# Further rounds of an expert with 32 slots instead of 64, in four column groups and four row groups of TensorE's array

## The chip, the cores and the metric

The kernel runs on one core of one Trainium2 chip. The metric is device time in microseconds (us) of one execution. Three runs of the kernel before gave 1126.19 (the median), 1116.86 and 1128.22 us.

## The reference

The program is one inference step of a two-layer decoder trunk on 320 tokens: 256 of a prompt and 64 of a sample group, with the same weights. Layer 0 has a Conformer convolution module and layer 1 multi-head latent attention. Each layer ends in a mixture of 16 experts, and each token goes to two of them:

```python
def moe(x, r_w, r_b, w1, w3, w2):
    t = x.reshape(-1, D_MODEL)                       # D_MODEL = 1024
    aff = jax.nn.sigmoid((t @ r_w).astype(jnp.float32))
    ...                                              # best group of 4, then the top 2 experts in it
    gates = ...                                      # 0 but for the two chosen experts of a token
    out = jnp.zeros(t.shape, jnp.float32)
    for e in range(N_EXPERTS):                       # 16
        h = jax.nn.silu(t @ w1[e]) * (t @ w3[e])     # 1024 -> 512, twice
        out = out + gates[:, e:e + 1] * (h @ w2[e]).astype(jnp.float32)
    return out.astype(x.dtype).reshape(x.shape)
```

All of it is in float32. The routing of these inputs, counted with the reference's own functions for prompt and sample together, gives the experts of layer 0 28, 43, 43, 52, 49, **65**, 53, 41, 52, 33, 15, 42, 34, 30, 40, 20 tokens, and those of layer 1 53, **68**, 35, 50, 55, 57, 36, 22, 49, 30, 19, 48, 35, 23, 40, 20.

## The kernel before

The kernel computes an expert on gathered tokens, `C = 64` slots at a time, with one instruction stream per engine written by hand and semaphores between them. **The first round** of an expert takes its first 64 tokens: POOL gathers the rows of x from HBM by an indirect DMA, PE turns them (`turn_rows`, L931, into the bank `TURN`), ACT copies them to SBUF (L692), PE makes the up products with w1 and w3 (`up`, L944: the product with w1 lies in partitions 0 to 63 of the bank `UP`, that with w3 in 64 to 127), ACT takes silu of the one half (L697), DVE multiplies by the other (L1353), PE turns the hidden rows (L931), DVE copies them (L1357), PE makes the down product (`down`, L952, into the bank `DOWN`: the columns 0 to 511 of the result in partitions 0 to 63, the others in 64 to 127), and DVE copies the result (L1362). Two experts share one put product (`put`, L987): a one-hot matrix with the gates in it, turned by PE, times the results, added onto the residual that stays in five PSUM banks (`TOTAL`) through all 16 experts.

**A further round** takes the next 64 tokens of an expert that has more. The routing on DVE counts the rounds of every expert (L1310 to L1326, the table `rounds`), and each engine's stream has after each expert a branch on that number and a loop (`further`, L999 on PE). The rounds use TensorE's matmuls of the first round on buffers of their own, with the same weights, and end with their own put product (L1022 and L1023) whose left side is one expert's one-hot rows in partitions 64 to 127. In the round everything is one chain: turn (L931), ACT copy (L710), up (L944), silu (L713), product (L1372), turn of the hidden rows (L931) and of the one-hot matrix (L1013), copy (L1374), down (L952), two copies (L1378), put (L987). Its gather (L556) is issued long before.

**What sets the order around it.** The weights of an expert are 6.3 MB: w1 and w3 (two DMAs, L416), w2 (one DMA, L419). They have two buffers, and a third one for expert 2 alone. SP's stream issues the DMAs of expert e+2 when the buffer of expert e is free, further rounds included: `load_over` (L436 to L442) waits for the last up product of e before it issues w1 and w3, and for the last down product before w2. All go into one queue in order. PE waits at L955 (`w13_ready`) for w1 and w3.

## Time and profile before

| | |
|---|---|
| runs | 1116.86, 1126.19, 1128.22 us |
| span of the profiled execution | 1117.9 us (the page gives no other time of its own) |
| PE busy | 980.2 us, 88% of the span |
| DVE, ACT, POOL busy | 336.2, 167.1, 104.3 us |
| chain that ended last | PE 71%, DMA 12%, DVE 8%, ACT 3% |
| read from HBM | 260.04 MB, of them about 200 MB expert weights |

A row of a group of instructions has the line in the kernel, engine, operation, what it writes and reads, the shape and the count, then the summed busy time and the mean duration of one.
### The profile page before, as it was taken

The numbers are of one execution on the slowest core, as the hardware profiler recorded it, in microseconds if no ns is written. First come the engines' busy times: TensorE is split into PE (matmuls) and PEld (weight loads), VectorE is DVE, ScalarE is ACT, GpSimd is POOL, SyncE is SP. The second block draws the span as 40 slices with busy tenths as digits, with TensorE's granted clock in tenths as the row PEclk, the third lists the DMA queues.
The fourth block names the chain that finished last, engine by engine and source line by source line (L and its number), as shares of the span: only waits on it lengthen the run. The fifth ranks groups of instructions, "written<-read, shape, count | busy, mean of one in ns | idle before, by whom it ended". The sixth has DMA issues, their size and how long they took to land.

```text
span 1117.9 us, 14216 instructions
## 1 busy us (share of the span) xinstructions
PE 980.2 (88%) x4754; PEld 485.2 (43%) x4755; DVE 336.2 (30%) x792; ACT 167.1 (15%) x327; POOL 104.3 (9%) x196
## 2 busy tenths in 40 slices
PE   3989979799989998968998888889798999989993
PEld 2756534543323343325655555444543334323331
DVE  1554445421121221142224433213521121211215
ACT  1000031211011110012122322220111011111001
POOL 2051000101000000014100023000010000000000
PEclk9989989699999999998898989989698999999997
DMA  8485261999969999978203110557385399999991
GB/s 215 121 291 155 59 258 58 341 364 367 367 233 319 377 376 378 392 252 279 73 6 96 53 55 24 190 203 285 131 278 197 146 324 376 382 379 373 385 353 48
DMA packets 131621, 267.18 MB, mean 239 GB/s; under 512 B 7386, under 2 KB 39158, under 8 KB 131555
## 3 DMA queue, kind: packets, MB, share of 16 engines
q1 hardware_dynamic: 121200, 237.75, 60.2%
q0 software_dynamic: 5392, 12.60, 4.3%
q10 hardware_dynamic: 4979, 16.15, 4.0%
q8 instruction: 33, 0.54, 0.2%
q14 instruction: 17, 0.14, 0.0%
HBM read 260.04 MB, written 7.15 MB: 239 GB/s over the span
## 4 chain that ended last, share of the span: by engine, by line
PE 71%; DMA 12%; DVE 8%; ACT 3%; SPq 2%; issue 2%; ACTq 0%; DVEq 0%
PE bank L944 19%; DMA w<-in_e_w 9%; PE bank L952 9%; PE wide L987 4%; PE bank L877 4%; PE bank L770 3%; PE bank L931 3%; PE wide L877 2%; PE wide L770 2%; PE wide L1708 2%; PE bank L786 2%; DMA w<-in_state_conv 2%; PE bank L1585 2%; DMA dbuf<-in_a_w_pw 2%; PE bank L1686 2%
## 5 line engine op out<-in xcount | busy, mean ns | idle before, releaser
L944 PE MATMUL bank<-w,dbuf 128*64 128x512 f32 x1024 | 234.0, 610 | 14.4 <-DMA w<-in_e_w 11.5
L944 PEld LDWEIGHTS bank<-w,dbuf 128*64 128x64 f32 x1024 | 78.9, 141 | 163.0 <-issue 160.8
L952 PE MATMUL bank<-w,dbuf 128*64 128x512 f32 x512 | 129.9, 653 | 11.0 <-DVE dbuf L1357 10.4
L1362 DVE COPY dbuf<-bank 64x512 f32<-64x512 f32 x64 | 44.1, 689 | 164.6 <-PE bank L952 164.2
L1353 DVE TENSOR_TENSOR dbuf<-dbuf,bank 64x512 f32<-64x512 f32 x32 | 22.1, 690 | 204.4 <-ACT dbuf L697 204.4
L697 ACT ACTIVATE dbuf<-bank 64x512 f32<-64x512 f32 x32 | 18.9, 591 | 418.2 <-PE bank L944 418.2
L952 PEld LDWEIGHTS bank<-w,dbuf 128*64 128x64 f32 x512 | 42.5, 148 | 81.4 <-issue 81.1
L987 PE MATMUL wide<-dbuf,ukT 128*128 128x512 f32 (+1 forms) x144 | 70.3, 615 | 6.0 <-DVE dbuf L1378 3.0
L931 PEld LDWEIGHTS bank<-ident,dbuf 64*128 64x128 f32 x476 | 41.3, 160 | 50.9 <-issue 41.7
L931 PE MATMUL bank<-ident,dbuf 64*128 64x64 f32 x476 | 50.6, 244 | 9.9 <-DVE dbuf L1362 3.4
L540 POOL COPY idx_col<-idx 64x1 int32 (+1 forms) x32 | 5.7, 179 | 572.5 <-PE bank L931 389.5
L527 POOL DMA_DIRECT2D w<-in_cache_kpe x64 | 34.3, 536 | 224.0 <-PE bank L1686 123.3
L770 PE MATMUL bank<-xT,dbuf 128*128 128x320 f32 x128 | 39.5, 471 | 3.8 <-DMA dbuf<-in_a_w_pw 3.8
L987 PEld LDWEIGHTS wide<-dbuf,ukT 128*128 128x128 f32 (+1 forms) x144 | 24.7, 189 | 30.5 <-issue 19.2
L770 PE MATMUL wide<-xT,dbuf 128*128 128x320 f32 x128 | 35.4, 435 | 0.0
L770 PEld LDWEIGHTS bank<-xT,dbuf 128*128 128x128 f32 x128 | 26.7, 210 | 16.0 <-DMA dbuf<-in_a_w_pw 4.3
L543 POOL DMA_INDIRECT dbuf<-x_rows,idx_col x32 | 29.9, 936 | 11.3 <-issue 11.3
L786 PE MATMUL bank<-w,ukT 128*32 128x256 f32 x512 | 29.3, 380 | 0.0
L770 PEld LDWEIGHTS wide<-xT,dbuf 128*128 128x128 f32 x128 | 24.1, 190 | 10.9 <-issue 1.2
L877 PE MATMUL bank<-dbuf,w 128*128 128x512 f32 (+1 forms) x64 | 23.4, 635 | 6.0 <-ACT w L620 6.0
L1357 DVE COPY dbuf<-bank 128x256 f32<-128x256 f32 x32 | 13.6, 425 | 40.2 <-PE bank L931 39.5
L692 ACT ACTIVATE dbuf<-bank 128x512 f32<-128x512 f32 x32 | 19.1, 597 | 42.3 <-PE bank L931 42.3
(352 smaller groups left out, 1115.1 us busy)
## 6 DMA issues: line engine op xcount, KB each, us to landing
w<-in_e_w SPq DMA_DIRECT2D x90, 2048.0 KB, 20.2
dbuf<-in_a_w_pw SPq DMA_DIRECT2D x16, 512.0 KB, 5.8
w<-u_rows SPq DMA_DIRECT2D x32, 142.0 KB, 3.0
dbuf<-in_a_w_pw ACTq DMA_DIRECT2D x1, 4096.0 KB, 17.8
dbuf<-in_e_w SPq DMA_DIRECT2D x2, 2048.0 KB, 14.9
w<-in_cache_ckv SPq DMA_DIRECT2D x32, 128.0 KB, 2.7
dbuf<-in_cache_ckv SPq DMA_DIRECT2D x32, 128.0 KB, 2.1
dbuf<-in_b_w_o SPq DMA_DIRECT2D x2, 2048.0 KB, 7.8
```

The source lines that it names most:

```text
L527: pool.dma_start(cpe[p % 2][:, bass.ds(it * 4 + n, 1)].rearrange("p o r -> p (o r)"), src)\
L543: nc.gpsimd.indirect_dma_start(xg[s], None, x_rows[l], bass.IndirectOffsetOnAxis(ap=idx_col[s][:], axis=0))\
L770: last = nc.tensor.matmul(B[2 * s + h][:, 0:T], pw1[s][:, k, h], xT[:, k], start=(k == 0), stop=(k == KD - 1))
L786: last = nc.tensor.matmul(B[6 + j % 2][32 * g:32 * g + 32, 0:SEQ], tap_w[j % 2][:, g, q], copies[j % 2][:, g, 4 * q:4 * q + SEQ], start=(q ...
L877: last = nc.tensor.matmul(dst, left[:, k, t0:t0 + m], w_out[:, k, h * 512:(h + 1) * 512], start=(k == 0), stop=(k == KD - 1))
L931: last = nc.tensor.matmul(bank[:, k * C:(k + 1) * C], src[:, k * P:(k + 1) * P], ident[r0:r0 + C, r0:r0 + C], start=True, stop=True, is_tr ...
L944: last = nc.tensor.matmul(bank[n * C:(n + 1) * C], x[:, k], w[n][k], start=(k == 0), stop=(k == KD - 1))
L952: last = nc.tensor.matmul(bank[n * C:(n + 1) * C], h[:, k], w[k][:, n * 512:(n + 1) * 512], start=(k == 0), stop=(k == 3))
L987: last = nc.tensor.matmul(TOTAL[i][h], left[:, t0:t0 + m], rows[:, h * 512:(h + 1) * 512], start=False, stop=stop)
L1362: last = V.tensor_copy(y_pair[s * C:(s + 1) * C, h * 512:(h + 1) * 512], DOWN[h * C:(h + 1) * C, :])
L1585: last = nc.tensor.matmul(B[h % 2][:, 0:T], wuq[:, k, h * 192:h * 192 + NOPE], cqT[:, k], start=(k == 0), stop=(k == 3))
L1686: last = nc.tensor.transpose(key_bank(n)[0:(P if n < 8 else ROPE), j * P:(j + 1) * P], src, ident[:])
```

## The change

A further round holds `H = 32` slots; the first round keeps 64. An expert with 65 to 96 tokens has one further round as before, one with 97 to 128 has two where it had one.

- **Up** (`up_more`): the 512 columns of w1 and of w3 are cut in halves, and each of the four quarters goes into a column group of its own, 32 of the array's columns wide: 32 matmuls of 256 moving columns instead of 16 of 512. w1's product lies in partitions 0 to 63 (half a in 0 to 31, half b in 32 to 63), w3's in 64 to 127.
- **Silu and product** are then on 64 x 256 instead of 64 x 512, the copy before the up product on 128 x 256 instead of 128 x 512.
- **Turn of the hidden rows** takes 2 matmuls instead of 4. DVE writes each turned block twice, side by side, so that the down product has 64 columns on its left side as before and gives each of its 32 rows twice.
- **Copy of the result**: the result's 512-column halves lie in partitions 0 to 63 and 64 to 127, each row twice, and are copied by one 128 x 512 instruction instead of two of 64 x 512.
- **Put** (`put_rows_more`): the one-hot matrix is built four times side by side (128 x 128 instead of 128 x 64, three instructions), turned into 128 partitions and copied, and each matmul of the put product takes 32 rows of it in a row group of its own; token tiles 0 and 1 and the two halves of the result have four different ones.
- **Routing** on DVE: up to 8 further rounds instead of 4 are counted, which is 4 more small instructions in each of two loops, and the matrices of slots are 6 x 8 x 16 instead of 6 x 4 x 16 (and 6 x 32 instead of 6 x 64).
- **The gather** of a further round has 32 rows.

```diff
+            def turn_more():
+                for k in range(KD):
+                    last = nc.tensor.matmul(TURN[:, k * H:(k + 1) * H], xg_more[:, k * P:(k + 1) * P], ident[0:H, 0:H],
+                                            start=True, stop=True, is_transpose=k > 0)
+                return last
+            def up_more(w):
+                for k in range(KD):
+                    for q in range(4):
+                        n, lo = q // 2, q % 2 * (FE // 2)
+                        last = nc.tensor.matmul(UP[q * H:(q + 1) * H, 0:FE // 2], xe_more[:, k],
+                                                w[n][k][:, lo:lo + FE // 2], start=(k == 0), stop=(k == KD - 1))
+                return last
+            def turn_hidden_more():
+                for c in range(2):
+                    last = nc.tensor.matmul(UP[:, c * C:(c + 1) * C], hid_more[:, c * P:(c + 1) * P],
+                                            ident[C:2 * C, C:2 * C], start=True, stop=True, is_transpose=c > 0)
+                return last
+            def down_more(w):
+                for k in range(4):
+                    for n in range(2):
+                        last = nc.tensor.matmul(DOWN[n * C:(n + 1) * C],
+                                                hT_more[:, k % 2 * 2 + k // 2].rearrange("p r t -> p (r t)"),
+                                                w[k][:, n * 512:(n + 1) * 512], start=(k == 0), stop=(k == 3))
+                return last
+            def put_rows_more():
+                for i, (t0, m) in enumerate(TILES):
+                    for h in range(2):
+                        r0 = (2 * h + i % 2) * H
+                        nc.tensor.matmul(TOTAL[i][h], put_more[r0:r0 + H, t0:t0 + m], y_more[r0:r0 + H],
+                                         start=False, stop=False)
...
-                        turn_rows(TURN, xg_more, KD).then_inc(m_turned, 1)
+                        turn_more().then_inc(m_turned, 1)
                         pe.wait_ge(m_copied, first + c)
-                        up(xe_more, UP, W13[w]).then_inc(m_up, 1)
+                        up_more(W13[w]).then_inc(m_up, 1)
                         pe.wait_ge(m_hid, first + c)
-                        turn_rows(UP, hid_more, 4, C).then_inc(m_ht, 1)
+                        turn_hidden_more().then_inc(m_ht, 1)
...
                         pe.wait_ge(m_htc, first + c)
-                        down(hT_more, DOWN, W2[w]).then_inc(m_down, 1)
+                        down_more(W2[w]).then_inc(m_down, 1)
                         pe.wait_ge(m_y, first + c)
                         pe.wait_ge(m_hotc, first + c)
-                        for p in range(PUTS):
-                            put(p, put_more, y_more)
+                        put_rows_more()
...
-            for q in range(2, CHUNKS):
-                after(V.scalar_tensor_tensor(chunk6, rank6, float(q * C), chunk6, ALU.is_ge, ALU.add))
+            for q in range(1, MORE):
+                after(V.scalar_tensor_tensor(chunk6, rank6, float(C + q * H), chunk6, ALU.is_ge, ALU.add))
...
-            for c in range(2, CHUNKS):
-                after(V.scalar_tensor_tensor(n16, cnt, float(c * C), n16, ALU.is_gt, ALU.add))
+            for c in range(1, MORE):
+                after(V.scalar_tensor_tensor(n16, cnt, float(C + c * H), n16, ALU.is_gt, ALU.add))
...
                         dve.wait_ge(m_act, first + c)
-                        V.tensor_tensor(hid_more, act_more, UP[C:2 * C], ALU.mult).then_inc(m_hid, 1)
+                        V.tensor_tensor(hid_more, act_more, UP[C:2 * C, 0:FE // 2], ALU.mult).then_inc(m_hid, 1)
                         dve.wait_ge(m_ht, first + c)
-                        V.tensor_copy(hT_more, UP[:, 0:4 * C].rearrange("p (k t) -> p k t", k=4))\
-                            .then_inc(m_htc, 1)
+                        V.tensor_copy(hT_more, UP[:, 0:2 * C].rearrange("p (b t) -> p b t", b=4).unsqueeze(2)
+                                      .to_broadcast([P, 4, 2, H])).then_inc(m_htc, 1)
                         dve.wait_ge(m_down, first + c + 1)
-                        for h in range(2):
-                            last = V.tensor_copy(y_more[:, h * 512:(h + 1) * 512], DOWN[h * C:(h + 1) * C, :])
-                        last.then_inc(m_y, 1)
+                        V.tensor_copy(y_more, DOWN[:, :]).then_inc(m_y, 1)
```

PE's stream in one further round (the branch that follows an expert whose weights lie in buffer 0), before:

```order
L931 MATMUL bank<-ident,dbuf 128x64 x8
L944 MATMUL bank<-w_0,dbuf 64x512 x16
L931 MATMUL bank<-ident,dbuf 128x64 x4
L1013 MATMUL bank<-ident,dbuf 64x128 x2
L1013 MATMUL bank<-ident,dbuf 64x64
L952 MATMUL bank<-w_0,dbuf 64x512 x8
L987 MATMUL wide<-dbuf,ukT 128x512 x4
L987 MATMUL bank<-dbuf,ukT 64x512 x2
```

and with the change:

```order
L941 MATMUL bank<-ident,dbuf 128x32 x8
L950 MATMUL bank<-w_0,dbuf 32x256 x32
L957 MATMUL bank<-ident,dbuf 128x64 x2
L1056 MATMUL bank<-ident,dbuf 128x128 x2
L1056 MATMUL bank<-ident,dbuf 128x64
L965 MATMUL bank<-w_0,dbuf 64x512 x8
L975 MATMUL wide<-dbuf,ukT 128x512 x4
L975 MATMUL bank<-dbuf,ukT 64x512 x2
```

The chain keeps its steps; the up product (L944, now L950) has twice the matmuls of half the columns each, and the put product (L987, now L975) the same number of the same width.

DVE's stream in the routing of a layer, from the count of rounds before the slot matrices to the count of rounds per expert, before:

```order
L1297 SCALAR_TENSOR_TENSOR dbuf<-dbuf 128x6 x3
L1298 RECIPROCAL dbuf<-dbuf 128x3
L1299 SCALAR_TENSOR_TENSOR dbuf<-dbuf 128x6
L1300 TENSOR_TENSOR dbuf<-route,dbuf 128x384
L1301 TENSOR_TENSOR ukT<-ukT,dbuf 128x48
L1302 TENSOR_TENSOR dbuf<-route,dbuf 128x6
L1303 TENSOR_TENSOR dbuf<-route,dbuf 128x24
L1306 TENSOR_TENSOR dbuf<-dbuf 128x24
L1307 TENSOR_TENSOR dbuf<-dbuf 128x384
L1310 TENSOR_SCALAR dbuf<-dbuf 128x16
L1312 SCALAR_TENSOR_TENSOR dbuf<-dbuf 128x16 x3
```

and with the change:

```order
L1341 SCALAR_TENSOR_TENSOR dbuf<-dbuf 128x6 x7
L1342 RECIPROCAL dbuf<-dbuf 128x3
L1343 SCALAR_TENSOR_TENSOR dbuf<-dbuf 128x6
L1344 TENSOR_TENSOR dbuf<-route,dbuf 128x192
L1345 TENSOR_TENSOR ukT<-ukT,dbuf 128x48
L1346 TENSOR_TENSOR dbuf<-route,dbuf 128x6
L1347 TENSOR_TENSOR dbuf<-route,dbuf 128x48
L1350 TENSOR_TENSOR dbuf<-dbuf 128x48
L1351 TENSOR_TENSOR dbuf<-dbuf 128x768
L1354 TENSOR_SCALAR dbuf<-dbuf 128x16
L1356 SCALAR_TENSOR_TENSOR dbuf<-dbuf 128x16 x7
```

Nothing changes its place: the two counting loops have 7 instructions instead of 3, and the slot matrices are 192 and 768 wide instead of 384 and 384.

## Rows read from the trace of the kernel before

**Rows 1.** The page: span of the profiled execution.

```profile
span 1117.9 us, 14216 instructions
```

**Rows 2.** Waits of PE: total us, times, longest.

```profile
PE bank L944 <- DMA w<-in_e_w: 11.5, 7, 3.8
```

**Rows 3.** Chain of waits, further round of layer 0: start us, us, what.

```profile
309.88 0.88 PE bank L931 x9
...
310.78 0.60 ACT dbuf L710
...
311.43 8.65 PE bank L944 x32
...
320.11 0.60 ACT dbuf L713
...
320.73 0.70 DVE dbuf L1372
...
322.61 3.68 PE bank L952 x16
...
327.02 0.69 DVE dbuf L1378
...
327.76 3.70 PE wide L987 x8
331.46 1.01 PE bank L987 x4
332.46 7.02 PE bank L944 x32
```

**Rows 4.** Chain of waits, up and down of the further round of layer 1.

```profile
847.78 10.12 PE bank L944 x32
...
860.43 5.37 PE bank L952 x16
```

**Rows 5.** Groups by shape: line, engine, operation, shape, count, busy us, mean ns, idle before.

```profile
L786 PE MATMUL bank<-w,ukT 128*32 128x256 f32 x512 | 29.3, 380 | 0.0
...
L701 ACT ACTIVATE ukT<-bank 128x320 f32<-128x320 f32 x16 | 7.0, 437 | 0.0
...
L1357 DVE COPY dbuf<-bank 128x256 f32<-128x256 f32 x32 | 13.6, 425 | 40.2 <-PE bank L931 39.5 <-issue 0.7
```

**Rows 6.** Windows: from:to us, length, busy per engine, PEclk, DMA share, GB/s.

```profile
310.00:321.00 11.00, 9.37 (x41) 3.15 (x41) 1.04 (x4) 1.19 (x2) 0.00 (x0) 0.84 0.13 50
...
338.00:341.00 3.00, 3.00 (x19) 1.51 (x16) 0.69 (x1) 1.19 (x2) 0.36 (x2) 1.00 0.26 53
341.00:426.00 85.00, 80.31 (x375) 31.91 (x373) 17.94 (x39) 11.02 (x16) 7.31 (x16) 0.98 1.04 367
847.00:859.00 12.00, 10.19 (x34) 2.88 (x32) 0.71 (x3) 1.19 (x2) 0.00 (x0) 0.72 0.01 3
876.00:896.00 20.00, 20.00 (x96) 7.50 (x92) 2.49 (x4) 1.66 (x3) 1.27 (x3) 1.00 0.06 16
896.00:1068.00 172.00, 159.88 (x726) 62.39 (x726) 34.17 (x74) 21.48 (x33) 12.79 (x30) 0.95 1.03 375
```

**Rows 7.** Timeline of SP, 316 to 345 us: issues of weight DMAs.

```profile
320.32 1.02 SPq L416 DMA_DIRECT2D w<-in_e_w  x2
...
339.67 1.00 SPq L416 DMA_DIRECT2D w<-in_e_w  x2
```

**Rows 8.** Chain of waits, layer 0: the one wait for weights after the round.

```profile
401.54 24.90 DMA w<-in_e_w
...
426.57 8.79 PE bank L944 x32
```

**Rows 9.** Timeline of DVE in the routing of layer 0.

```profile
213.10 0.56 DVE L1307 TENSOR_TENSOR dbuf<-dbuf 128x384 f32<-128x384 f32 x1
...
213.77 0.59 DVE L1312 SCALAR_TENSOR_TENSOR dbuf<-dbuf 128x16 f32<-128x16 f32 x3
```

**Rows 10.** Timeline of PE in the same stretch: the product for further slots.

```profile
217.71 1.33 PE L916 MATMUL bank<-dbuf 128*64 128x64 f32 x12
```

More of the change, by code:

```diff
@@ L47 @@
 C = 64
-CHUNKS = T // C
+H = C // 2
+MORE = (T - C) // H
 BIG = 1e30
@@ L237, in trunk_step @@
         chunk6, rest6, slot6 = (part(dbuf, R0 + 712 + 6 * n, 6) for n in range(3))
-        of_chunk = part(dbuf, R0 + 730, 6, CHUNKS - 1)
+        of_chunk = part(dbuf, R0 + 1344, 6, MORE)
         gate_sum = part(dbuf, R0 + 754, 3)
         hot = part(dbuf, R0 + 768, 6, C)
-        hot_rest = part(dbuf, R0 + 1152, 6, C)
-        right_rest = part(dbuf, R0 + 1536, 6, CHUNKS - 1, E)
+        hot_rest = part(dbuf, R0 + 1152, 6, H)
+        right_rest = part(dbuf, R0 + 1536, 6, MORE, E)
         top_at = sb("top_at", [P, 3, 8], mybir.dt.uint32)
@@ L547, in further @@
             def further(e):
-                count = pool.value_load(rounds[0:1, 0, bass.ds(e, 1)], min_val=0, max_val=CHUNKS - 1)
+                count = pool.value_load(rounds[0:1, 0, bass.ds(e, 1)], min_val=0, max_val=MORE)
                 first = pool.value_load(rounds[0:1, 1, bass.ds(e, 1)], min_val=0, max_val=ROUNDS_MAX)
@@ L704, in further @@
                 act.wait_ge(cnt_set, l + 1)
-                count = act.value_load(rounds[0:1, 0, bass.ds(e, 1)], min_val=0, max_val=CHUNKS - 1)
+                count = act.value_load(rounds[0:1, 0, bass.ds(e, 1)], min_val=0, max_val=MORE)
                 first = act.value_load(rounds[0:1, 1, bass.ds(e, 1)], min_val=0, max_val=ROUNDS_MAX)
@@ L709, in further @@
                         act.wait_ge(m_turned, first + c + 1)
-                        nc.scalar.activation(xe_more, TURN[:, :].rearrange("p (k t) -> p k t", k=KD), ACT.Copy)\
+                        nc.scalar.activation(xe_more, TURN[:, 0:KD * H].rearrange("p (k t) -> p k t", k=KD), ACT.Copy)\
                             .then_inc(m_copied, 1)
                         act.wait_ge(m_up, first + c + 1)
-                        nc.scalar.activation(act_more, UP[0:C], ACT.Silu).then_inc(m_act, 1)
+                        nc.scalar.activation(act_more, UP[0:C, 0:FE // 2], ACT.Silu).then_inc(m_act, 1)
                         act.wait_ge(m_hot, first + c)
-                        nc.scalar.activation(put_more, TURN[0:C, 0:T], ACT.Copy).then_inc(m_hotc, 1)
+                        nc.scalar.activation(put_more, TURN[:, 0:T], ACT.Copy).then_inc(m_hotc, 1)
                 with act.Else():
@@ L999, in further @@
             def further(e, w):
-                count = pe.value_load(rounds[0:1, 0, bass.ds(e, 1)], min_val=0, max_val=CHUNKS - 1)
+                count = pe.value_load(rounds[0:1, 0, bass.ds(e, 1)], min_val=0, max_val=MORE)
                 first = pe.value_load(rounds[0:1, 1, bass.ds(e, 1)], min_val=0, max_val=ROUNDS_MAX)
@@ L1288, in dve_experts @@
             mark(V.scalar_tensor_tensor(rank1, rank, 1.0, mask, ALU.add, ALU.mult))
-            after(V.tensor_scalar(chunk6, rank6, float(C), None, ALU.is_ge))
+            after(V.tensor_scalar(chunk6, rank6, float(C), 1.0, ALU.is_ge, ALU.add))
             after(V.tensor_tensor(gates, mask, aff, ALU.mult))
@@ L1336, in build, with build_more @@
                 return last
+            def build_more(c, e):
+                for i in range(3):
+                    V.tensor_scalar(hot_more[:, i],
+                                    route[:, bass.ds(c * H + (R_IOTA + 1 + H), H)].unsqueeze(1).to_broadcast([P, 4, H]),
+                                    rank1[:, i, bass.ds(e, 1)], gates[:, i, bass.ds(e, 1)], ALU.is_equal, ALU.mult)
             def build_pair(e, n):
@@ L1365, in further @@
             def further(e):
-                count = dve.value_load(rounds[0:1, 0, bass.ds(e, 1)], min_val=0, max_val=CHUNKS - 1)
+                count = dve.value_load(rounds[0:1, 0, bass.ds(e, 1)], min_val=0, max_val=MORE)
                 first = dve.value_load(rounds[0:1, 1, bass.ds(e, 1)], min_val=0, max_val=ROUNDS_MAX)
```

50 lines of the change are left out of this document (27 added, 23 removed).

## The prediction

> **What bounds the kernel now.** I started from the page: the profiled execution spans 1117.9 us [rows 1], close to the lowest run (1116.86), 8 us under the median (1126.19). A further round runs twice in it. The counts of the routing say where: one expert of layer 0 (65 tokens) and one of layer 1 (68) have more than 64, none over 96. So there are two further rounds before and two after, with one and four tokens in them.
>
> Next, the chain of waits through the round of layer 0 [rows 3]: it is serial. PE turns, ACT copies, PE multiplies, and so on; no other expert's work lies between, so every piece saved moves the next expert's up product forward. The round lasts from 309.88 to 332.46 us, 22.6 us. That of layer 1 has the same pieces, with two longer matmul stretches [rows 4].
>
> Third, who is behind PE: the DMA queue with the weights. PE waits for it only 7 times, 11.5 us in all [rows 2], but the windows show it full: 367 and 375 GB/s at a share of 1.03 or more in 341 to 426 and 896 to 1068 us [rows 6]. It is idle in the further rounds, because the full buffers are not released before the round's up product has ended: a share of 0.13 in 310 to 321 us, 0.01 in 847 to 859, and also 0.06 in 876 to 896 [rows 6]. In layer 0 the chain then passes once through the weights: 24.90 us of DMA, on which the up product at 426.57 us waits [rows 8]. So a shorter round counts only as far as the loads behind it start earlier as well.
>
> **The change in the round, piece by piece.**
> - *Turn*, 0.88 us [rows 3]: nine matmuls as before, of fewer columns, each with a weight load of 128 columns: 0. Bounds 0 and -0.3.
> - *Copy by ACT*: 0.60 us for 512 columns [rows 3], 0.437 for 320 [rows 5]; the line through both gives 0.38 for 256. -0.2.
> - *Up*: 64 instructions of 256 columns. The convolution runs exactly this shape in four column groups at 29.3 / 512 = 57 ns from one to the next, though each is 380 ns under way [rows 5]: 64 x 57 = 3.7 us. Before it is 7.02 at the full clock (the next expert's, [rows 3]), but 8.65 here and 10.12 in layer 1 [rows 3, 4], since TensorE is granted 1.2 GHz at first, after a stretch with short turns and waits. The excess is half of the time at the low level: 3.3 and 6.2 us, which the granted clocks 0.84 of 11 us and 0.72 of 12 us bear out (3.5 and 6.7) [rows 6]. If the low level lasts as long as now, the new product does 1.65 of its 3.7 us of work in 3.3 and ends at 5.3; in layer 1 it does 3.1 in 6.2 and ends at 6.8. Both times -3.3.
> - *Silu and product*: 0.60 and 0.70 [rows 3]; half the columns cost about 0.39 on ACT by the same line and 0.43 on DVE (its copy of 256 columns, [rows 5]). -0.5.
> - *Turn of the hidden rows*: five instructions become three. -0.15.
> - *Down*: as many of the same shape, 3.68. 0. In layer 1 it takes 5.37 for the clock [rows 4]; whether the low level falls on it again is open: bounds -1.7 and +3.7.
> - *Copy of the result*: two of 0.69, one after the other [rows 3], become one. -0.7.
> - *Put*: 3.70 us for eight instructions of 128 columns on the left, 1.01 for four of 64 [rows 3]. No row of the trace has two row groups at work at once. The bounds are 0 (they go one after the other) and a quarter of the eight's time, 0.93. The nearest row is the four column groups, which overlap fully [rows 5], so I take 0.93; the last four overlap in pairs already and stay. -2.8.
>
> The Trainium skill ("TensorE: Matmul & The Clock Gate", section "Measured speedup vs the span model") gives 3.07 times for four row groups and 2.38 for three column groups, less than the count. With 3.07 the put would be 1.2 instead of 0.93, and the sum 0.5 us smaller over the two rounds; for column groups the trace's 57 ns speaks against such a loss.
>
> Sum of a round: 0.2 + 3.3 + 0.5 + 0.15 + 0.7 + 2.8 = **7.7 us**.
>
> **What of it arrives.** Layer 1: the queue is idle from 876 us to the release by the up product that ends at about 895 us [rows 6], so the loads start 7.7 earlier, and everything behind shifts with them: 7.7. Layer 0: the next expert's loads are issued at 320.32, when the round's up product ends, and the next ones at 339.67 [rows 7]. The queue works off the first until about 338.8 (a share of 0.26 in the 3 us from 338, [rows 6]) and starts again at 341. Now the first begin 3.5 earlier (copy and up alone) and end at 335.3; the second are issued at 332.0 and queue behind. From 341 on the queue was full up to the wait at 426.57, so that point moves by 341 - 335.3 = **5.7**, and PE, 7.7 early, waits 2 us longer there. Together 13.4.
>
> **The routing** gets eight more small DVE instructions of about 0.2 us (three take 0.59, [rows 9]), a slot matrix twice as wide (+0.45 on 0.56, [rows 9]) and one half as wide (-0.25): +1.0 before the slot matrices are ready, +1.8 in all. PE takes them up at 217.71 [rows 10] and they are ready at 213.66: 4 us of cover. The counts reach the streams about 1 us later, but the first load that waits for them also waits for the first up product, 8 us on. Cost 0; without that cover 1 us a layer. The product itself has twice the columns in half as many rows of output, at 1.33 us [rows 10] limited by its weight loads: +0 to +1. Three wider instructions for the one-hot matrix and a 32-row gather lie beside the up product or long before it: 0.
>
> **Forecast.** 1126.19 - 13.4 = 1112.8, or 1104.5 from the profiled execution. I say **1113**.
>
> **Rivals.**
> - *The row groups take turns* (0.18). The put stays at 4.7; a round saves 4.9, in both layers (layer 0 would pass on up to 5.7). 9.8: 1116.4. For it: no row shows the overlap. Against: the column groups do.
> - *The clock takes it back* (0.14). The new round has bursts of 5 us between the same waits, and transposes. If the 1.2 GHz last through it, the up product costs 7.3 in both layers (-1.35 and -2.8), down 7.3 (+3.6 and +1.9), put 3.9 (-0.8), the rest -1.5: about 0 in layer 0 and -3.2 in layer 1: 1123. For it: the fall at the start of both up products; against: the clock returned within them.
> - *Slower* (0.05): the low level lasts on through the next expert's up product, +7.0 in each layer [rows 3], place: 332 and 872 us. Sum 7 in layer 0 and 3.8 in layer 1: 1137. It decides once the low level lasts 15 us longer than now in a round, since each us costs a half and 7.7 are saved. The skill's same page (part 4) says that transposes do not count as busy, which would help this case; in the trace the level fell after such turns, but rose in the up product.
> - *The weights keep more of it* (part of the first case's width): if layer 0 moves only by the 3.5 of the first release, 11.2 in all: 1115.
> - *Nothing else differs*: a second further round for an expert with over 96 tokens would cost 15 us; the counts exclude it.
> - My forecast: 0.55. The remaining 0.08 are for scatter and what I overlooked.
>
> **Range.** Low: 1104.5 less about 2 for bounds (turn, down) is 1102. High: the clock's 1123. About 1 in 10 lies beyond each. The runs before scatter by 11 us, so a difference under 1% (11.3 us) can't be told from none. The forecast's 13.4 is just above: of its 0.55 I put 0.42 on faster; of the row groups' 0.18, 0.05; of the rest 0.02. Faster 0.49, slower 0.08 (the slow case, 0.03 of scatter), same 0.43.
>
> **What would show it.** In the changed trace: 64 up instructions in 5 to 7 us; the eight of the put product starting in groups of four; one DVE copy of 128 x 512; the queue idle for less in the rounds, without the gap at 338 to 341; a longer wait of PE at the expert that now starts at 426.57. I am wrong if the down product or the next up product shows the low clock, if the round is not about 15 us, or if PE waits for the slot matrices at 217 us.

## The result, and the profile after

| | before | after |
|---|---|---|
| median (lowest to highest), four runs each | 1121.53 us (1113.41 to 1128.22) | 1102.17 us (1099.08 to 1105.37) |
| profiled execution: time, span | none given, 1117.9 us | 1105.37 us, 1103.7 us |
| mean granted clock of the profiled execution | 0.931 | 0.935 |

The ratio is 0.984, with an interval of 0.981 to 0.988: 17.6 us faster (13.6 to 21.6). The two medians alone differ by 19.4. Forecast were 13.4 us and 1113 us, counted from a median of three runs, 1126.19; with a fourth run the median of the kernel before is 1121.53. The change ran twice more, unaltered, beside the kernel before: 1102.66 against 1120.76 us, and 1102.14 against 1120.93 us, 18.1 and 18.8 us. So the gain is larger than forecast by 4 to 5.5 us. Of the 10.8 us between 1113 and 1102.17, another 4.7 are the kernel before, whose median came out lower.

Two lines of the page after answer to [rows 1] and to the table of the engines' busy times:

```profile
span 1103.7 us, 14350 instructions
...
PE 963.1 (87%) x4814; PEld 480.5 (44%) x4815; DVE 337.7 (31%) x806; ACT 166.3 (15%) x327; POOL 104.5 (9%) x196
```

PE is busy 17.1 us less than before (980.2). The chain of waits through the round of layer 0 is the answer to [rows 3] (start, us, what):

```profile
310.71 1.01 PE bank L941 x9
311.75 0.39 ACT dbuf L713
312.18 6.58 PE bank L950 x64
318.78 0.39 ACT dbuf L716
319.19 0.44 DVE dbuf L1423
319.67 0.49 PE bank L957 x3
...
320.73 3.62 PE bank L965 x16
324.38 0.70 DVE dbuf L1428
325.13 1.14 PE wide L975 x8
326.27 1.00 PE bank L975 x4
```

The chain has the same steps, and almost each is shorter. From the turn to the next expert's up product (at 327.27) it is 16.6 us, where it was 22.6. The up product went from 8.65 to 6.58, the eight put instructions from 3.70 to 1.14, the copy of the result from two instructions to one, and the down product stayed. The same view of layer 1, where [rows 4] had 10.12 and 5.37:

```profile
844.85 3.71 PE bank L950 x64
...
850.53 3.62 PE bank L965 x16
854.18 0.70 DVE dbuf L1428
854.93 1.14 PE wide L975 x8
```

Here both products run at the full clock, and the round is 13.5 us instead of 25.7. The windows say so too (from:to, length, busy per engine, granted clock, DMA share, GB/s); they answer to the ones of [rows 6]:

```profile
312.00:321.00 9.00, 7.85 (x72) 3.72 (x74) 0.85 (x2) 0.73 (x3) 0.00 (x0) 0.67 0.09 20
334.00:341.00 7.00, 7.00 (x32) 3.20 (x32) 1.11 (x2) 1.19 (x2) 1.29 (x3) 1.00 1.03 392
341.00:420.00 79.00, 75.34 (x357) 29.93 (x353) 16.57 (x34) 11.03 (x16) 6.46 (x15) 0.98 1.04 375
844.00:849.00 5.00, 4.04 (x71) 2.24 (x69) 0.60 (x4) 0.76 (x2) 0.00 (x0) 1.00 0.05 17
```

The granted clock over the up product is 0.67 in layer 0 and 1.00 in layer 1, with the same code. The gap of the weight queue at 338 to 341 us is gone (share 1.03 from 334 on), and the full stretch behind moves 375 GB/s where it moved 367. This profile had started the experts 0.83 us later (first up product of layer 0 at 221.45 instead of 220.62 us), so that much is to be added to what comes earlier in layer 0. The issues of weights that were at 320.32 and 339.67 [rows 7] come at 318.99 and 334.48, that is 2.2 and 6.0 us earlier:

```profile
318.99 1.02 SPq L419 DMA_DIRECT2D w<-in_e_w  x2
...
334.48 1.01 SPq L419 DMA_DIRECT2D w<-in_e_w  x2
```

The expert that waited at 426.57 [rows 8] starts at 420.87 (PE's timeline; in brackets the wait ahead and what ended it), 5.7 us earlier, or 6.5 with the 0.83:

```profile
403.61 7.09 PE L987 MATMUL bank<-w,dbuf 128*64 128x512 f32 x32 [0.40 <-DMA w<-in_e_w]
420.87 7.09 PE L987 MATMUL bank<-w,dbuf 128*64 128x512 f32 x32 [2.18 <-DMA w<-in_e_w]
...
454.12 8.78 PE L987 MATMUL bank<-w,dbuf 128*64 128x512 f32 x32 [2.57 <-DMA w<-in_e_w]
```

The 24.90 us of [rows 8] are a DMA on the chain; PE itself waited 3.29 us ahead of the product at 426.57, its only wait for weights in layer 0 behind the round. Now there are four, of 0.40, 2.18, 0.60 and 2.57 us, 5.75 together, and the product behind the last of them has the low clock (8.78) that stood at 426.57 before. In the whole program PE waits nine times for weights, 15.8 us, where [rows 2] had seven and 11.5:

```profile
PE bank L987 <- DMA w<-in_e_w: 15.8, 9, 4.3
```

The product for further slots, 1.33 us at 217.71 [rows 10], now starts 0.3 later and lasts half a microsecond longer; the slot matrix of [rows 9] takes 0.96 instead of 0.56. Timelines of PE and DVE:

```profile
218.03 1.84 PE L919 MATMUL bank<-dbuf 128*32 128x128 f32 x12
```

```profile
214.35 0.96 DVE L1351 TENSOR_TENSOR dbuf<-dbuf 128x768 f32<-128x768 f32 x1
...
215.43 1.43 DVE L1356 SCALAR_TENSOR_TENSOR dbuf<-dbuf 128x16 f32<-128x16 f32 x7
```

### The profile page after: what moved, and what is told of

The parts are those of the page before. It is cut to its first block, busy times and chain, and to the rows that moved or that the text cites. A ratio compares the mean times of both kernels' runs of the same rounds, so it can differ in the third digit from the quotient of the medians.

```text
span 1103.7 us, 14350 instructions
## 1 busy us (share of the span) xinstructions
PE 963.1 (87%) x4814; PEld 480.5 (44%) x4815; DVE 337.7 (31%) x806; ACT 166.3 (15%) x327; POOL 104.5 (9%) x196
## 4 chain that ended last, share of the span: by engine, by line
PE 68%; DMA 13%; DVE 9%; SPq 5%; ACT 4%; issue 2%; ACTq 0%; DVEq 0%
PE bank L987 16%; DMA w<-in_e_w 9%; PE bank L995 7%; PE bank L880 4%; PE wide L1030 4%; PE bank L773 3%; SPq L419 3%; PE wide L880 2%; PE wide L773 2%; PE wide L1757 2%; PE bank L934 2%; DMA w<-in_state_conv 2%; PE bank L789 2%; DMA dbuf<-in_a_w_pw 2%; PE bank L1634 2%
## 5 line engine op out<-in xcount | busy, mean ns | idle before, releaser
L987 PE MATMUL bank<-w,dbuf 128*64 128x512 f32 x960 | 217.7, 607 | 17.3 <-DMA w<-in_e_w 15.8
L987 PEld LDWEIGHTS bank<-w,dbuf 128*64 128x64 f32 x960 | 74.0, 140 | 156.4 <-issue 156.1
L995 PE MATMUL bank<-w,dbuf 128*64 128x512 f32 x480 | 117.4, 633 | 10.9 <-DVE dbuf L1408 10.9
L995 PEld LDWEIGHTS bank<-w,dbuf 128*64 128x64 f32 x480 | 38.9, 144 | 74.0 <-issue 74.0
L1030 PE MATMUL wide<-dbuf,ukT 128*128 128x512 f32 x128 | 62.9, 617 | 3.0 <-DVE dbuf L1413 3.0
L934 PEld LDWEIGHTS bank<-ident,dbuf 64*128 64x128 f32 x448 | 38.9, 160 | 41.4 <-issue 36.8
L934 PE MATMUL bank<-ident,dbuf 64*128 64x64 f32 x448 | 47.6, 244 | 3.6 <-DVE dbuf L1404 3.1
L1030 PEld LDWEIGHTS wide<-dbuf,ukT 128*128 128x128 f32 x128 | 21.8, 189 | 22.9 <-issue 16.3
L1408 DVE COPY dbuf<-bank 128x256 f32<-128x256 f32 x32 | 13.6, 425 | 40.2 <-PE bank L934 40.2
```

Source lines behind the costliest of these rows:

```text
L934: last = nc.tensor.matmul(bank[:, k * C:(k + 1) * C], src[:, k * P:(k + 1) * P], ident[r0:r0 + C, r0:r0 + C], start=True, stop=True, is_tr ...
L987: last = nc.tensor.matmul(bank[n * C:(n + 1) * C], x[:, k], w[n][k], start=(k == 0), stop=(k == KD - 1))
L995: last = nc.tensor.matmul(bank[n * C:(n + 1) * C], h[:, k], w[k][:, n * 512:(n + 1) * 512], start=(k == 0), stop=(k == 3))
L1030: last = nc.tensor.matmul(TOTAL[i][h], left[:, t0:t0 + m], rows[:, h * 512:(h + 1) * 512], start=False, stop=stop)
```

## The experiments

Each kernel was timed in five rounds beside the kernel before on the same chip. Times are medians, and ratios are to the kernel before. In the kernel after, a round waits first for DVE's copy of the expert's first-round result (`y_copied`), then turns, then waits for ACT's copy: between the last down product and the round's up product PE works about 1 us in 3. This is called the pause below.

### The change again (e1_again, h2_again)

> The changed kernel unaltered, against the kernel before on the same chip, as the yardstick of the runs beside it. Theory A (the rounds themselves): the two profiles differ by 14.2 us, of it 6.0 in the round of layer 0 and 12.2 in that of layer 1; the gain is 14 to 18 us, ratio 0.984 to 0.988. Theory B (a lucky draw of four runs, the kernel before scatters from 1113 to 1128): nearer to the 9 to 13 us that my pieces give, ratio 0.988 to 0.992.

> The changed kernel unaltered, as the yardstick of h3_early: 1101 to 1105 us. Theory A (in the changed kernel the low clock falls on the up product of layer 0 mostly, and on that of layer 1 seldom): its profile shows 6.5 us in layer 0 and 3.7 in layer 1. Theory B (the profiles so far were chance): any other pair.

Measured: 1102.66 us, ratio 0.983 (0.980 to 0.985), and 1102.14, 0.983 (0.979 to 0.987). The low clock does not fall the same way each time. The up product takes, in layer 0 and layer 1, 6.58 and 3.71 us in the first profile, 6.5 and 6.43 in the second, 5.35 and 6.43 in the third. The timelines of PE of the second and of the third show it for layer 1 (start, us; what it waited for in brackets), and the window over the first of the two rows has a granted clock of 0.56:

```profile
842.75 6.43 PE L950 MATMUL bank<-w,dbuf 128*32 128x256 f32 x64 [0.47 <-ACT dbuf L713]
```

```profile
842.74 6.43 PE L950 MATMUL bank<-w,dbuf 128*32 128x256 f32 x64 [0.47 <-ACT dbuf L713]
```

```profile
842.70:849.20 6.50, 6.43 (x64) 2.82 (x64) 0.00 (x0) 0.00 (x1) 0.00 (x0) 0.56 0.01 3
```

So the 3.7 us of layer 1 in the first profile were not what the change gives every time, and h2's expectation of 6.5 and 3.7 us failed. Of twelve new rounds in the profiles that have this pause and this up product (those of e3, f4, g3 and g4 below included), seven had the low clock over it and five had not. The down product at 5.37 us [rows 4] never came back: 3.6 to 3.7 in every profile of the new round.

The low clock also falls outside the rounds, and not always on the same product. In h2 it fell on the first up product of layer 0, which took 7.09 us in the profiles of before, after and e1:

```profile
220.15 8.79 PE L987 MATMUL bank<-w,dbuf 128*64 128x512 f32 x32 [0.78 <-ACT dbuf L695]
```

The round of layer 0 then began 90.96 us after that product's start, where it was 89.3 in the kernel before and in the two other profiles of the change. So what h2's round gained by its shorter up product (5.35, where e1 had 6.51) had been lost ahead of it.

### Column groups in pairs (e2_up_pairs, g2_early_pairs)

```diff
-                for k in range(KD):
-                    for q in range(4):
+                for half in range(2):
+                    for k in range(KD):
+                        for n in range(2):
+                            q, lo = 2 * n + half, half * (FE // 2)
...
```

> The up product of a further round with the same 64 instructions, in an order in which only two column groups are at work at a time: its rate is that of the kernel before. Theory A: the up product takes about 7 us at the full clock instead of 3.7, layer 1 loses 3.3 us whole and layer 0 up to 3.3, together 5 to 7 us slower than e1_again. Theory B (what the product costs is set by the low clock and hidden behind the weights): under 3 us.

> e4_early_turn, in which the clock stays up in the further rounds, with the up product in two column groups at a time as in e2_up_pairs. Theory A (the column groups are worth their 2.6 us per round once the clock does not hide it): 4 to 6 us slower than e4_early_turn's 1098.5, at 1102.5 to 1104.5. Theory B (they are worth nothing at the end): the same as e4_early_turn.

Measured: 1105.49 us, 2.8 more than the change in the same call, and, on top of the early turn below, 1101.83, 3.4 more than that alone, in another call. The up product lasts 6.27 us at the granted clock 1.00 in the window of e2 (the first row), and as long in the timeline of g2:

```profile
311.00:317.30 6.30, 6.27 (x64) 3.29 (x64) 0.00 (x0) 0.00 (x0) 0.00 (x0) 1.00 0.00 1
```

```profile
309.41 6.27 PE L951 MATMUL bank<-w,dbuf 128*32 128x256 f32 x64 [0.47 <-ACT dbuf L713]
```

Four groups in turn take 3.66 at this clock, so the overlap of four is real: 2.6 us a round, 5.2 in all. At the end the medians show about 3, less than both theories A had said. For e2 this is no surprise: in the profile of the unaltered change from the same call the up products had the low clock and took 6.51 and 6.43 us, no less than the pairs' 6.27 at the full one. Both of e2's rounds had the pause and kept the full clock. The intervals of the ratios (0.982 to 0.988 against 0.980 to 0.985, and 0.980 to 0.987 against 0.977 to 0.982) overlap, so the 3 are a size, not a proof. Note that the order of the instructions alone decides it: the same 64 instructions, in pairs, take 6.27 us, and the 32 wide ones of the old product took 7.02 at the full clock.

### Row groups in turn and in pairs (e3_put_serial, f4_put_pairs)

```diff
-                for i, (t0, m) in enumerate(TILES):
-                    for h in range(2):
-                        r0 = (2 * h + i % 2) * H
+                for h in range(2):
+                    for i, (t0, m) in enumerate(TILES):
+                        r0 = 2 * h * H
```

f4 has only the last line of it, so that neighbours are in two different groups.

> The put product of a further round with the same instructions, all of one half of the result in one row group: nothing overlaps. Theory A: its twelve instructions take 5 to 5.3 us instead of 2.14, so 3 us later per round: 3 in layer 1, 1 to 3 in layer 0, 4 to 6 slower than e1_again. Theory B (the weights hold layer 0 anyway): 3 us.

> The changed kernel with the put product of a further round in two row groups instead of four, overlapping in pairs. By overlap alone the eight instructions take 1.8 to 2.0 us instead of 1.14, so 1.5 to 2 us more in both rounds together. Theory A (in e3_put_serial the low clock came from only a quarter of the array's rows at work at a time, and cost most of the 16 us): here, with half of them, the clock stays and the loss against the changed kernel is 1 to 3 us, at about 1105 us. Theory B (it came from leaving four row groups at all, or from anything else in that order): near e3_put_serial, 1115 us or more.

Measured: e3 1118.72 us, 16.1 more than the change in the same call, far outside the 3 to 6 expected, and f4 1106.22, 3.6 more than the change's 1102.66, which is from another call. e3's rows on PE's timeline, and windows over its two put products:

```profile
324.10 1.98 PE L975 MATMUL wide<-dbuf,ukT 32*128 32x512 f32 x4 [0.79 <-DVE dbuf L1428]
326.01 1.07 PE L975 MATMUL bank<-dbuf,ukT 32*64 32x512 f32 x2
327.00 3.58 PE L975 MATMUL wide<-dbuf,ukT 32*128 32x512 f32 x4
330.52 1.97 PE L975 MATMUL bank<-dbuf,ukT 32*64 32x512 f32 x2
332.41 9.58 PE L987 MATMUL bank<-w,dbuf 128*64 128x512 f32 x32
```

```profile
324.10:332.40 8.30, 8.30 (x12) 2.10 (x12) 1.41 (x6) 0.00 (x0) 0.00 (x0) 0.69 1.02 372
860.60:869.40 8.80, 8.80 (x12) 2.28 (x12) 1.41 (x6) 0.00 (x0) 0.00 (x0) 0.64 1.05 401
```

The put product was expected at 5 to 5.3 us and took 8.3. Its first half took 2.90 at the full clock, so that 5.8 would be the whole at that clock (an estimate, twice the half). The second half took 5.4, at a granted clock of 0.52 over 327.0 to 332.4, with PE busy 100% of the window. The next expert's up product then took 9.58 instead of 7.09. Against the 2.14 and 7.09 us of the change that is 6.2 and 2.5 us in layer 0, and 6.7 and 1.9 in layer 1 (8.80 in the second window, 9.03 for the up product behind it). The sum is 17.3, and 16.1 are measured. By the estimate some 7 of it are the lost overlap (twice 5.8 less 2.14) and 10 the clock. f4's rows, in pairs:

```profile
322.38 1.99 PE L975 MATMUL wide<-dbuf,ukT 32*128 32x512 f32 x8 [0.79 <-DVE dbuf L1428]
324.29 1.07 PE L975 MATMUL bank<-dbuf,ukT 32*64 32x512 f32 x4
```

The eight take 1.99 in pairs and 1.14 in fours; one after the other, four alone take 1.98 at the full clock. The old eight took 3.70 [rows 3]. These rows are from layer 0, where the clock stayed at 1.00. In layer 1 of f4 it fell on the four instructions behind the eight and on the next expert's up product, which took 8.3 us instead of 7.0, again with PE busy all the time:

```profile
854.00:857.00 3.00, 3.00 (x8) 0.61 (x10) 0.00 (x0) 0.00 (x0) 0.00 (x0) 0.58 1.05 398
```

So f4's theory A, that pairs keep the clock, held in one of two rounds, and its loss of 3.6 us is a little more than the 1 to 3 expected. The overlap is what the put term rests on, and without it, with what the clock then takes, the change is worth 2 us (ratio 0.997, 0.995 to 0.9995), not the 9.8 of the first rival.

### The turn before the wait (e4_early_turn, h3_early, f1_before_early)

```diff
-                        pe.wait_ge(y_copied, e + (g0 + 1))
                         pe.wait_ge(m_xg, (first + c) * 16)
                         turn_more().then_inc(m_turned, 1)
...
                         pe.wait_ge(m_htc, first + c)
+                        pe.wait_ge(y_copied, e + (g0 + 1))
                         down_more(W2[w]).then_inc(m_down, 1)
```

The wait protects the bank that the down product writes, so it can stand there. f1 is the same edit on the kernel before.

> The changed kernel with one wait of PE moved: a further round's turn no longer waits until the first round's result has been copied, only its down product does. The turn and the copy by ACT then lie beside DVE's two copies, and PE has no pause of 1.7 us before them. Theory A: a round is 1.7 us shorter, and with the pause the low clock at the up product goes as well (6.6 us in the profile of layer 0, 3.7 in layer 1): 3 to 6 us faster than e1_again. Theory B (the clock falls at the turns, whatever the pause): 2 to 3.5 us faster.

> e4_early_turn once more, beside h2_again. Theory A (pause and low clock both go): 4 to 7 us faster than h2_again. Theory B (e4_early_turn was a lucky draw): under 3 us.

> The kernel before with only the one wait moved that e4_early_turn moved (a further round's turn does not wait for the copies of the first round's result). Theory A (much of a further round's price before is the low clock that follows the pause): 1.7 us less per round by the pause, and the up products at the full clock, 1.6 and 3.1 us less, in layer 1 perhaps 1.7 of the down product too: 6 to 10 us faster than the kernel before. Theory B (the change's gain is the number of TensorE's and DVE's columns, not the clock): 3.4 us.

Measured: 1098.45 us, ratio 0.979 (0.977 to 0.982), and again 1098.44, 0.980 (0.976 to 0.984): 4.2 and 3.7 less than the change in the same calls. f1: 1111.8, 0.990 (0.985 to 0.994), 12 less than the kernel before and more than the 6 to 10 that the theory of the clock gave it; its interval, 6 to 17 us, holds these too. e4 on PE's timeline:

```profile
306.79 0.84 PE L941 MATMUL bank<-ident,dbuf 32*128 32x32 f32 x9
...
308.10 3.66 PE L950 MATMUL bank<-w,dbuf 128*32 128x256 f32 x64 [0.47 <-ACT dbuf L713]
```

The wait of 1.67 us ahead of the turn is gone, and the up product is at the full clock in both layers, in f1 too (7.09). So the low clock of the up product hangs on the pause: the kernels that take it out or fill it had the full clock in twelve rounds of twelve (both layers of e4, h3, f1, g2, and of g1 and h1 below). With the pause it was none of four old rounds and seven of fourteen new ones, e2's two among them. This is the fastest version, 22 us under the kernel before; that it beats the change rests on two pairs of medians that agree, while the intervals of the ratios overlap.

### The pause filled (g1_fill, h1_before_fill)

```diff
                         pe.wait_ge(xe_copied, ...)
+                        for k in range(2):
+                            for n in range(2):
+                                nc.tensor.matmul(UP[n * C:(n + 1) * C], ident[:, 0:C], W13[w][n][k], start=True, stop=True)
                         pe.wait_ge(y_copied, e + (g0 + 1))
```

The four products are overwritten unread. They lie in the pause and are meant to take nothing from it, so that only the clock differs (in g1 the turn starts 5.3 us after the first round's down product, as in the kernel before). g1 is on the kernel after, h1 on the one before.

> The changed kernel with four matmuls more (eight instructions, about 1.8 us) in the pause of TensorE before a further round's turn, into a bank that the up product overwrites. The chain itself gets 0.1 to 0.2 us longer per round. Theory A (the pause of 1.7 us and the turns after it bring the low clock on the up product): the up products of both rounds run at the full clock, 3.7 us, and the kernel is up to 3 us faster per round that had it, 2 to 4 us in all. Theory B (the clock falls for other reasons): no change, or 0.3 us slower, and an up product of 6.5 us in layer 0 as in every profile of the changed kernel so far.

> The kernel before with the same four extra matmuls (1.8 us) in the pause before a further round's turn as in g1_fill. The chain gets 0.1 to 0.2 us longer per round and nothing else changes but the clock. Theory A (the low clock in the two rounds costs the kernel before 1.6 us in layer 0 and 3.1 + 1.7 us in layer 1, and it is this that my sum kept): 4 to 7 us faster than the kernel before, both up products at 7.1 us. Theory B (the missing 4 to 6 us come from somewhere else, such as the put product or the weights): within 2 us of the kernel before.

Measured: g1 1100.75 us, ratio 0.981 (0.978 to 0.985), h1 1118.61, 0.999 (0.996 to 1.002). On g1's timeline:

```profile
309.14 1.92 PE L1050 MATMUL bank<-w,ident 128*64 128x512 f32 x8
310.99 0.84 PE L941 MATMUL bank<-ident,dbuf 32*128 32x32 f32 x9
312.30 3.66 PE L950 MATMUL bank<-w,dbuf 128*32 128x256 f32 x64 [0.47 <-ACT dbuf L713]
```

and on h1's, in layer 1:

```profile
843.44 1.92 PE L1007 MATMUL bank<-w,ident 128*64 128x512 f32 x8
...
846.85 7.09 PE L944 MATMUL bank<-w,dbuf 128*64 128x512 f32 x32 [0.69 <-ACT dbuf L710]
...
856.49 5.25 PE L952 MATMUL bank<-w,dbuf 128*64 128x512 f32 x16
```

The mechanism holds: with the pause filled, the up products run at the full clock in both layers, 3.66 in one kernel and 7.09 in the other. Down stays at 5.25 in layer 1 of h1, so there the old round loses the clock a second time behind the up product, where PE waits 1.4 us for silu and product (0.60 and 0.70 in [rows 3]); the new round's wait there is 0.95. That this wait is the cause was not tried apart, and it isn't enough by itself: f1 has the same 1.42 us, and its down products took 3.65. But the size fails: the rounds of h1 are shorter by 1.5 and 3.1 us, and of the 4.6 only 2.3 arrive by the medians and 1.1 by the ratio (its interval just reaches 4.5). In layer 0 the trace shows where it went: the round began 1.3 us later after the layer's first up product, because an up product ahead of it was interrupted and took 1.3 us longer, by a gap for which the profile shows no reason (one of 1.30 us stands at the same place in g1):

```profile
280.71 5.37 PE L944 MATMUL bank<-w,dbuf 128*64 128x512 f32 x23 [0.74 <-issue]
```

Whether the fill brings this gap is not shown. No other profile has it in this product, but one without the fill has a longer one in layer 1 (f3, 2.34 us).

### One layer's further round left out (f2, f3, g3, g4)

```diff
+            never = 10 * T if l == 0 else 0        # l == 1 in f3 and g4
-            after(V.tensor_scalar(n16, cnt, float(C), None, ALU.is_gt))
+            after(V.tensor_scalar(n16, cnt, float(C + never), None, ALU.is_gt))
```

and the same number in the loop below it. f2 and f3 are the kernel before without the round of layer 0 and without that of layer 1, g3 and g4 the kernel after. They leave out the one token over 64 in layer 0, or the four in layer 1.

> The kernel before with no further round in layer 0: it leaves out the one token over 64 of one expert there. 22.6 us of chain are gone. Theory A (a saving in layer 0 arrives up to what the weight queue was idle, about 9.5 us in the round and 2.2 after it): 10 to 14 us faster than the kernel before. Theory B (it all arrives): 22 us.

> The kernel before with no further round in layer 1: it leaves out the four tokens over 64 of one expert there. 25.8 us of chain are gone, and the weight queue was idle for over 30 us before it is full. Theory A (all of it arrives): 22 to 26 us faster than the kernel before. Theory B (the weights keep a part here too): under 18.

> The changed kernel with no further round in layer 0: it leaves out the one token over 64 of one expert there. Against f2_before_none0 (1105.3) it shows what the change gains in layer 1 alone. Theory A (all that the round of layer 1 saves arrives, 9 to 12 us by the profiles): 1094 to 1096. Theory B (the weights keep a part, or the gain lies in layer 0): 1098 or more.

> The changed kernel with no further round in layer 1: it leaves out the four tokens over 64 of one expert there. Against f3_before_none1 (1097.4) it shows what the change gains in layer 0 alone. Theory A (5.7 to 7 us of the 6.0 to 7.7 arrive): 1090 to 1092. Theory B (the weights take most of it back): 1094 or more.

| | without layer 0's round | without layer 1's round |
|---|---|---|
| before | 1105.34, 0.986 (0.981 to 0.991) | 1097.42, 0.978 (0.974 to 0.983) |
| after | 1094.23, 0.974 (0.971 to 0.978) | 1087.49, 0.969 (0.965 to 0.973) |
| what the change saves in the round that is left | layer 1: 11.1 us; by ratios 13.3 | layer 0: 9.9 us; by ratios 10.8 |

Of the old rounds, 22.6 and 25.7 us long, 15.6 to 18.5 and 24 to 26 arrive: in layer 1 the round counts in full, in layer 0 the weights may keep a part, but less than f2's theory A had said (10 to 14 us arriving). g4 is 2.5 us under the range that it was given. Each saving is a difference between two kernels whose own ratios are uncertain by 0.4 to 0.5%, 4 to 5 us, so that the saving is uncertain by some 6. So these times place neither layer against the forecast's 7.7 and 5.7; the two savings also add up to 21, more than the whole gain.

The traces divide it further. From PE's timelines I took, for every execution with a round in the layer, the time from the layer's first expert up product to the mark at its end (layer 0: the first product of layer 1's attention; layer 1: the end of the span). The mark of layer 0 after, which stood at 504.88 us before:

```profile
502.45 6.18 PE L1597 MATMUL wide<-dbuf,xT 128*128 128x320 f32 x16 [6.14 <-ACT xT L669]
```

| us | old round | new round |
|---|---|---|
| experts of layer 0 | before 284.3, f3 284.1 | after 281.0, e1 279.8, h2 279.0, g4 277.4 |
| experts of layer 1 | before 299.9, f2 303.7 | after 288.5, e1 292.8, h2 292.1, g3 289.5 |
| between the two | before 313.1, f3 313.2 | after 312.7, e1 and h2 313.8 |

The means differ by 4.9 us in layer 0 and by 11.1 in layer 1, and nothing is saved between. With h1's fill the two layers take 284.7 and 300.4. In layer 0 the 1.5 us of the round are gone in the gap shown above. In layer 1 the time behind the round is 246.0 us in before, 249.8 in f2 and 249.5 in h1, so that one execution can't show 3.1. The early turn of h3 and e4 takes 273.1 and 273.0 in layer 0, about as little as g3 without any round (272.6; f2 269.8).

For layer 0, the windows show what became of the cap at the wait of 426.57. The first is f3 (the old round), the second g4 (the new one):

```profile
341.00:425.00 84.00, 79.67 (x374) 31.73 (x372) 17.58 (x38) 11.02 (x16) 6.95 (x16) 0.98 1.04 370
```

```profile
332.00:416.00 84.00, 78.48 (x374) 31.21 (x373) 18.35 (x41) 11.02 (x16) 7.25 (x16) 1.00 1.04 377
```

The queue shows the share 1.04 in both and moves 370 GB/s in one and 377 in the other, so the share of 1.04 was not yet its limit. The expert behind the stretch starts at 425.75 in f3 and at 416.79 in g4, 9.0 us earlier, all that g4's shorter round gives (22.5 less 13.5). Of that 6.8 are left at the layer's end. The rest is lost later than forecast, in PE's wait of 3.94 us for weights at 416.79 (3.12 at 425.75 in f3) and in the product behind it, at the low clock for longer (9.94 us against 8.78).

## Why the prediction was wrong in size

The direction, the place and the mechanism were right: the rounds became shorter, by the pieces named, and the time came through. The sum of 13.4 us was too small against the 17.6 to 18.8 measured. For the same reason 1113 was too high, and also because the forecast started from 1126.19, 4.7 us above the median of the four runs. The prediction's own note that the profiled execution stood 8 us under that median pointed there.

**Pieces that held.** In the first profile the steps of layer 0's round, from one's start to the next's, became shorter by: turn with ACT's copy 0.08 us (0.2 forecast), silu and product 0.5 (0.5), turn of the hidden rows 0.13 (0.15), copy of the result 0.70 (0.7), put 2.56 (2.8). The eight put instructions took 1.14 us, between the bounds of 3.70 and 0.93 and near the lower one, a factor of 3.2 on 3.70. The Trainium skill ("TensorE: Matmul & The Clock Gate", section "Measured speedup vs the span model") has 3.07 times for four row groups, and the trace agrees with it rather than with my 4. For three column groups it has 2.38; no run here has three, and the 64 up instructions in four stood 57 ns apart (3.66 / 64), the convolution's distance, so the loss of which the prediction spoke did not come.

**The term that failed: up and down in layer 1, through the clock.** The prediction said "if the low level lasts as long as now" and took 3.3 us of up and 0 of down in each layer. It did not last as long as before. From the durations (half of the time at the low level is excess over 3.66), it lasted 5.7, 5.7, 3.4 and 0 us in layer 0 (up 6.5, 6.5, 5.35 and 3.66 in after, e1, h2 and g4) and 0, 5.5, 5.5 and 0 in layer 1 (3.66, 6.43, 6.43, 3.66 in after, e1, h2 and g3), where it had been 3.3 and 6.2 with the old round. On average up saves 3.1 us in layer 0, near the 3.3, but 5.1 in layer 1, where 3.3 had been taken; and down, whose low clock in layer 1 never came back, saves the 1.7 that had stood in the bounds alone. The rounds of layer 1 are shorter by 12.2, 9.2, 9.2 and 12.2 us (10.7 on average), not 7.7, and the layer's experts by 11.1. That f2's old round has the same 10.1 and 5.35 as [rows 4] says that the long low level of the old round was not one execution's. How much of it the new round keeps is chance from one execution to the next: up saved 6.4 us in two of the four and 3.7 in the other two. Why the level comes back sooner in the new round is not shown.

**The cap of layer 0: right in size, wrong in place.** Its rounds are shorter by 6.0, 6.1, 7.5 and 9.1 us, and 4.9 on average are left at the layer's end, where 5.7 had been forecast. But the step "that point moves by 341 - 335.3 = 5.7" did not bind: at 426.57 the first profile had moved 6.5 and g4 9.0. In the first profile the first loads were released only 2.2 us earlier, not 3.5, because the up product before them had the low clock. That the point still moved by 6.5 comes from the queue: it lost its gap of 2.2 us (338.8 to 341), and over some 83 us it moved 375 instead of 367 GB/s, worth 1.8 us by these rates (an estimate); the prediction had taken the rate of the full queue as fixed. Afterwards 2.3 to 3.3 us were lost again. So that 4.9 is near 5.7 is partly luck.

**What stays open.** 4.9 + 11.1 = 16.0 against 17.6, 18.1 and 18.8 leaves 1.6 to 2.8 us. They lie within what single executions scatter: two with the old round of layer 1 differ by 3.8 us, the three profiled executions of the change took 3 to 5 us more than its medians, and the spans of the first pair differ by only 14.2. Open is also why a fill gains 1 to 2 us on the old kernel, while the early turn, which does the same to the clock and takes the wait of 1.68 us from the chain twice, gains 12; in f1's profiled execution the two layers are shorter by 1.5 and 5.4 us, 6.9 together.

**The rivals.** *The row groups take turns*: no, four instructions start within 20 ns, and the next four again (at 325.127 to 325.147 and 325.661 to 325.681 us). e3 made them take turns, and that costs 16.1 us, not the 3.6 between the rival and the forecast: its price had 4.7 us for the put product, which is 5.8 one after the other, and left out that the clock fell in it. *The clock takes it back* and *slower*: no, in no profile of the unaltered change did the round's down product or the next up product show the low clock. In e3 the next up product did in both layers and in f4 in layer 1, so the slower case can happen; it needed a put product of one row group at a time, or of two. *The weights keep more*: 4.9 instead of 5.7 in layer 0, inside the width given. *Routing*: the way from the slots' first product on PE (L904, now L907) to the first expert's up product became 0.25 us longer in layer 0 and 0.44 in layer 1, within the 0 to 1 given, and PE did not wait for DVE there.

## What to carry to other kernels

Small products that take the array's row and column groups in turn are worth their full factor only in that order of issue. Pairs gave back 2.6 of 3.4 us in the up product and 0.85 of 2.56 in the put product, and one row group after the other lost more than all of it, since the clock fell as well. Look at every pause of PE of some microseconds ahead of a long product, for the product may pay for it in the clock; move the wait behind independent work, which also shortens the chain, rather than fill it. Count such a gain at the end of the program and not in the product: the low clock can fall on another product instead. A forecast from the median of a few runs inherits their scatter, here 4.7 us. A full DMA queue caps a gain, but a share of 1 in the profile does not fix its rate: at 1.04 it moved 367 to 377 GB/s here.

## What the runs showed of the hardware that I had not expected

- The granted clock fell while PE was busy 100% of the time: 0.69 and 0.64 over the two put products of e3, in which matmuls on 32 rows ran one after the other (8.3 and 8.8 us, where 5.8 is the estimate from the first half at the full clock), and the next product on 128 rows began at the low level (9.58 instead of 7.09 us). With two groups in turn (f4) the eight took 1.99 us, but in layer 1 the granted clock over the 3 us behind them was 0.58, with PE busy all the time.
- Whether the new up product after the pause had the low level for 5.7 us, for 3.4 or not at all differed from execution to execution of the same kernel (6.43, 5.35, 3.66 us). With the pause taken out or filled the up product ran at the full clock in all five kernels that had this: 3.66 us in fours, 6.27 in pairs, 7.09 in the old shape.
- Twelve matmuls of 128 moving columns into 32 rows took 1.84 us [rows 10 had 1.33 for 64 columns into 64 rows]: 153 ns each where 111 were needed.
